# The output norm of a gated-DeltaNet layer in two groups of heads, and the first two output tiles fed head by head

## The reference, cut to what matters

```python
o, s_new = _gated_delta_chunked(q, k, v, g, beta, s0)          # 8 heads of 128
o = _rms_norm(o.astype(h.dtype), o_norm) * jax.nn.silu(gate.reshape(bsz, t_len, H_A, DV))
return o.reshape(bsz, t_len, H_A * DV) @ w_out, new_conv, s_new.astype(h.dtype)
# the caller: x = x + y, then the norm of x and the FFN
```

## Time and profile before

| | |
|---|---|
| median of 3 runs | 2751.65 us |
| the three runs | 2749.22, 2751.65, 2757.39 us |
| the profiled execution | 2749.38 us |
| its span from first to last instruction | 2747.6 us |
| mean granted clock of TensorE | 0.992 |
| busy: TensorE, weight loads, VectorE, ScalarE, GpSimd | 98%, 95%, 48%, 34%, 11% |

### The profile page before, as it was taken

One profiled execution on the slowest core, in us unless ns is written; L12 is line 12 of the kernel. 1 busy time (PEld: TensorE's weight loads), 2 busy tenths in 40 slices (PEclk: granted clock), 3 DMA queues, 4 the chain that ended last, 5 costly groups with the idle time before them and its releaser, 6 DMA issues.

```text
span 2747.6 us, 52338 instructions
## 1 busy us (share of the span) xinstructions
PE 2702.4 (98%) x22041; PEld 2609.8 (95%) x22041; DVE 1327.1 (48%) x1715; ACT 921.6 (34%) x1384; POOL 292.2 (11%) x348
## 2 busy tenths in 40 slices
PE   8999999999999999999999999999999999999999
PEld 8999999998887999999999999999986699999999
DVE  4434347765555643333564343434547754343354
ACT  4222124454323332222342222212348732122243
POOL 2000002211224100000110000000133210000011
PEclk9999999999999999999999999999999999999999
DMA  5223222221012232323222332322303422232321
GB/s 141 77 80 88 77 80 88 87 82 30 20 34 76 83 92 77 92 77 89 84 78 85 121 113 77 92 77 84 105 18 108 142 74 84 82 86 78 87 92 54
DMA packets 308138, 225.96 MB, mean 82 GB/s; under 512 B 8270, under 2 KB 301567, under 8 KB 307967
## 3 DMA queue, kind: packets, MB, share of 16 engines
q1 hardware_dynamic: 307280, 224.26, 27.1%
q0 software_dynamic: 576, 0.00, 0.0%
q10 hardware_dynamic: 162, 0.04, 0.0%
HBM read 212.14 MB, written 12.13 MB: 82 GB/s over the span
## 4 chain that ended last, share of the span: by engine, by line
PE 95%; DVE 3%; issue 1%; ACT 1%; POOL 1%; DVEq 0%; POOLq 0%; ACTq 0%
PE ps L537 80%; PE ps L2445 1%; PE ps L556 1%; PE ps L2411 1%; PE ps L1810 1%; PE ps L2453 1%; PE ps L2350 1%; PE ps L1814 1%; PE ps L1558 0%; PE ps L2595 0%; PE ps L2447 0%; PE ps L2448 0%; DVE w_lo L489 0%; PE ps L1660 0%; PE ps L1833 0%
## 5 line engine op out<-in xcount | busy, mean ns | idle before, releaser
L537 PE MATMUL ps<-hx_hi,w_lo 128*128 128x320 f32 (+1 forms) x3730 | 1096.5, 294 | 0.0
L537 PE MATMUL ps<-hx_lo,w_hi 128*128 128x320 f32 (+1 forms) x3730 | 1096.0, 294 | 0.0
L537 PE MATMUL ps<-hx_hi,w_hi 128*128 128x320 f32 (+1 forms) x3730 | 1089.6, 292 | 1.6 <-DVE w_lo L489 1.3
L474 ACT ACTIVATE w_hi<-raw 128x1024 fp32r<-128x1024 f32 (+1 forms) x362 | 375.4, 1037 | 1216.9 <-PE ps L537 1216.2
L537 PEld LDWEIGHTS ps<-hx_hi,w_hi 128*128 128x128 f32 x3730 | 700.2, 188 | 4.7 <-DVE w_lo L489 2.5
L537 PEld LDWEIGHTS ps<-hx_hi,w_lo 128*128 128x128 f32 x3730 | 700.2, 188 | 0.0
L537 PEld LDWEIGHTS ps<-hx_lo,w_hi 128*128 128x128 f32 x3730 | 699.0, 187 | 0.3
L537 PE MATMUL ps<-hid_hi,w_hi 128*128 128x320 f32 (+1 forms) x1920 | 566.5, 295 | 2.2 <-DVE hid_lo L2239 0.5
L537 PE MATMUL ps<-hid_lo,w_hi 128*128 128x320 f32 (+1 forms) x1920 | 567.6, 296 | 0.0
L537 PE MATMUL ps<-hid_hi,w_lo 128*128 128x320 f32 (+1 forms) x1920 | 561.3, 292 | 0.0
L489 DVE TENSOR_TENSOR w_lo<-raw,w_hi 128x1024 fp32r<-128x1024 f32 (+1 forms) x362 | 460.9, 1273 | 108.7 <-ACT w_hi L474 108.6
(11 more groups left out here) (500 smaller groups left out, 2316.7 us busy)
## 6 DMA issues: line engine op xcount, KB each, us to landing
raw<-in_ffn_w_in SPq DMA_DIRECT2D x176, 512.0 KB, 5.0
raw<-in_ffn_w_out SPq DMA_DIRECT2D x64, 512.0 KB, 4.1
raw<-in_a_w_in SPq DMA_DIRECT2D x33, 512.0 KB, 4.6
raw<-in_ffn_w_out SPq DMA_DIRECT2D x32, 384.0 KB, 3.5
raw<-in_ple_w_gate SPq DMA_DIRECT2D x8, 1024.0 KB, 5.2
raw<-in_w_kv SPq DMA_DIRECT2D x16, 512.0 KB, 4.1
k_page<-in_cache_k SPq DMA_DIRECT2D x16, 512.0 KB, 3.6
v_page<-in_cache_v SPq DMA_DIRECT2D x14, 512.0 KB, 4.7
```

What stands on the lines that cost most here:

```text
L474: nc.scalar.activation(w_hi[:, m, 0:k], s.view(m, slot), ACT.Copy).then_inc(w_hi_done, 1)
L537: last = nc.tensor.matmul(TILE[m][:, c0:c1], w[:, m, k], h[:, k, c0:c1], start=k == 0 and a == 0, stop=k == k_all - 1 and a == 2)
```

## The change

The norm's sums, roots, reciprocals and scales are made for the two groups of heads one after the other, with buffers of their own (`std_c`, `rs_c`, `inv`, the sums' banks). For the first group, the sums are taken in the last level of the last pair, and everything up to the scales within the last scan. The second group follows behind the scan. The update of state 7 writes banks 2 and 5 and waits for the first group's scales where it waited for state 3. The table of the square root is loaded ahead of the last pair's first level. The first two tiles of the output product are fed head by head by `first_products`: a block of tile 0 and a block of tile 1 as the heads come, with transposes and spreads of the second group between them. VectorE's order is written out to match. The 15 matmuls of `keep_warm`, in three calls, become one call with 6. `tail_products` goes.

```diff
-        ... "vnt3_s os3_s upd6_s vnc3_s vnm3_s osum3_s vnm7_s upd3_s upd7_s orec0 orec1 ilo0 ilo1")
+        ... "vnt3_s os3_s orec_a0 orec_a1 upd6_s vnc3_s vnm3_s osum3_s vnm7_s upd3_s ilo_a0 ilo_a1 upd7_s "
+            "orec_b0 orec_b1 ilo_b0 ilo_b1")
...
+        O_SUMS = [[ps[:, b, 0:HC] for b in banks] for banks in ((2, 5), (6, 7))]
+        SPREAD_BANK = (4, 5, 4, 5, 7, 4, 5, 7)
+        O_TOKEN_BANK, O_ROWS_BANK, O_TOKEN_COL = (5, 6), (5, 7), 256
...
 # SyncE
-            after(sp, "su3_s")
+            after(sp, "om3_s")
             load_unit(sp, plan[plan.index(s) + 1], 0, 0)
-            states_out(3)
+            states_out(3, last_state_out)
             after(sp, "su7_s")
             load_unit(sp, plan[plan.index(s) + 1], 0, 1)
-            states_out(7, last_state_out)
+            states_out(7, stored)
...
 # ScalarE
+                if hp == NG - 1:
+                    nc.scalar.preload_act_table_set("sqrt_and_others")
...
+                    if (hp, level) == (NG - 1, LEVELS - 1):
+                        output_sums_read(0)
...
                         o_square(2)
+                        output_roots(0)
+                    if (hp, i) == (NG - 1, 2):
+                        after(act, "osum3_s")
+                        o_square(3)
+                        output_scales_high(0)
...
+            output_high(0, "n0", "s0")
+            output_sums_read(1)
+            split_hi(act, (next_step, 0, 0), 1)
+            output_high(1, "n1", "s0")
+            output_roots(1)
+            output_high(4, "n4", "s4")
+            output_scales_high(1)
+            output_high(5, "n5", "s4")
+            for h in LAST_SUMS:
+                output_high(h, f"n{h}", f"s{h // 4 * 4 + 2}")
...
 # VectorE
+                    if (hp, i) == (3, 3):
+                        sample_update(3)
+                        output_scales_low(0)
...
                     if (hp, i) == (3, 1):
+                        output_reciprocals(0)
                         sample_update(6)
...
+            output_samples(0, 3, 0)
+            output_samples(4, 3, 2 * TS)
+            output_normed(0)
             split_lo(dve, (next_step, 0, 0), 0)
+            output_normed(1)
+            output_low(0)
+            output_normed(4)
+            output_low(1)
+            split_lo(dve, (next_step, 0, 0), 1)
+            output_reciprocals(1)
+            output_normed(5)
+            output_low(4)
+            output_scales_low(1)
+            output_low(5)
+            output_normed(2)
+            output_samples(2, 6, 0)
+            output_samples(6, 6, 2 * TS)
+            output_normed(3)
+            output_low(2)
+            output_normed(6)
+            output_low(3)
+            output_normed(7)
+            output_low(6)
+            output_low(7)
...
 # TensorE, between the tiles of the product
+        def first_products(pe, s):
+            n, base = s.n["unit"], s.n["hid"] - KD
+            blocks = {m: 0 for m in range(2)}
+            def block(m, h):
+                pe.wait_ge(w_lo_done, 2 * n + m + 1)
+                if m:
+                    pe.wait_ge(g["of"], of_count["s4"])
+                    after(pe, "upd7_s")
+                pe.wait_ge(hid_done, base + SQUARED.index(h) + 1)
+                for c0, c1 in PARTS:
+                    for a, (w, x) in enumerate(((w_hi, hid_hi), (w_lo, hid_hi), (w_hi, hid_lo))):
+                        last = nc.tensor.matmul(TILE[m][:, c0:c1], w[:, m, h], x[:, h, c0:c1],
+                                                start=blocks[m] == 0 and a == 0, stop=blocks[m] == KD - 1 and a == 2)
+                blocks[m] += 1
+                if blocks[m] == KD:
+                    last.then_inc(tile_done, 1)
+            block(0, 0)
+            block(0, 1)
+            output_scale_rows(pe, 1)
+            block(0, 4)
+            block(1, 0)
+            block(1, 1)
+            after(pe, "ostd_b1")
+            sample_norm_spread(pe, 1, 6)
+            norm_spread(pe, 4)
+            block(0, 5)
+            block(1, 4)
+            norm_spread(pe, 5)
+            block(1, 5)
+            norm_spread(pe, 6)
+            block(0, 2)
+            block(1, 2)
+            norm_spread(pe, 7)
+            for h in (3, 6, 7):
+                for m in range(2):
+                    block(m, h)
...
 # TensorE, in the last pair
                         sample_update(2, 2)
+                        output_sums(pe, 0)
...
                         sample_read(3)
+                        output_by_token(pe, 0)
                         sample_update(2, 6)
...
                         sample_update(3, 3)
+                        output_scale_rows(pe, 0)
                     if (hp, i) == (3, 3):
-                        after(pe, "osum3_s")
-                        output_sums(FIRST_SUMS, 0)
                         sample_update(3, 7)
-            output_sums(LAST_SUMS, 1)
-            keep_warm(pe, 3, 0)
...
+            sample_norm_spread(pe, 0, 3)
             norm_spread(pe, 0)
-            sample_norm_spread(pe)
-            for h in range(1, 5):
-                norm_spread(pe, h)
+            after(pe, "upd7_s")
+            norm_spread(pe, 1)
+            after(pe, "upd3_s")
+            output_sums(pe, 1)
+            norm_spread(pe, 2)
+            output_by_token(pe, 1)
+            norm_spread(pe, 3)
+            keep_warm(pe, 6, 0)
...
-            tail_products(pe)
```

More of the change, by code:

```diff
@@ L1208, in gdn_act @@
             act.wait_ge(g["ocp"], PT * HA)
-            after(act, "osum2_s", "osum3_s")
-            for h in (3, 6, 7):
+            for h in (6, 7):
                 o_square(h)
-            act.wait_ge(g["osum"], 2)
-            done("osums", nc.scalar.activation(halves(o_sums[:]), O_SUMS, ACT.Copy))
             next_step = plan[plan.index(s) + 1]
-            after(act, "su7_s")
             split_hi(act, (next_step, 0, 0), 0)
[L1217 to L1229, removed]
+            output_high(0, "n0", "s0")
[6 more added lines that the diff above has]
+            output_high(5, "n5", "s4")
+            for h in LAST_SUMS:
+                output_high(h, f"n{h}", f"s{h // 4 * 4 + 2}")
         def gdn_dve(dve, s):
@@ L1535, in sample_norm_spread, with output_sums @@
                                         start=True, stop=True)
-            done("o_sample_scales", last)
+            done(f"o_samples_{'ab'[n]}", last)
+        of_count.update((name, n + 1) for n, name in enumerate("s0 s4 n0 n1 n4 n5 n2 s2 s6 n3 n6 n7".split()))
+        og_count = {h: n + 1 + n // 4 for n, h in enumerate(SQUARED)}
+        def output_sums(pe, n):
+            pe.wait_ge(g["osq"], 4 * n + 4)
+            for half in range(2):
+                for x, h in enumerate((FIRST_SUMS, LAST_SUMS)[n]):
+                    last = nc.tensor.matmul(O_SUMS[n][half][32 * x:32 * x + 32], hot[:, 15 - h:47 - h], osq[h][:, half * HC:(half + 1) * HC],
+                                            start=True, stop=True)
+            last.then_inc(g["osum"], 1)
@@ new lines, in output_by_token, with output_scale_rows @@
+        def output_by_token(pe, n):
+            x = "ab"[n]
+            after(pe, f"osums_{x}")
+            for i in range(NT):
+                rows_, c0 = x_rows_of(i), O_TOKEN_COL + HA * i
+                last = nc.tensor.matmul(bank(O_TOKEN_BANK[n])[0:rows_, c0:c0 + HA], o_sums[:, i * P:i * P + rows_], e32[:, 0:HA],
+                                        start=True, stop=True)
+            done(f"o_by_token_{x}", last)
+        def output_scale_rows(pe, n):
+            x = "ab"[n]
+            after(pe, f"orec_{x}0", f"orec_{x}1")
+            nc.tensor.transpose(bank(O_ROWS_BANK[n])[0:32, 0:P], rs_c[n][:, 0:PT * HA], ident[:])
+            done(f"o_scale_rows_{x}", nc.tensor.transpose(bank(O_ROWS_BANK[n])[0:HA, P:P + TS], rs_c[n][0:TS, PT * HA:], ident[0:TS, 0:TS]))
@@ L1819, in gdn_pe @@
                     after(pe, f"zero{a}")
+                    if hp == NG - 1:
+                        after(pe, "osums_a")
                     for i in range(PT):
```

204 lines of the change are left out of this document (98 added, 106 removed).

## The result

The changed kernel took 2757.0 us at the median of 12 runs (2753.11 to 2761.79), the kernel before 2752.38 (12 runs on the same chip). The ratio is 1.0019, with a 95% interval of 1.0010 to 1.0027: 4.6 us, or 0.19%, slower. That lies inside the 0.3% that were named as no change and got the highest chance, but on the other side of the old time from the forecast of 2749.8, and on the upper end of its range. The profiled execution of the changed kernel took 2757.05 us, 1.7 us more than its span.

What follows compares the result with a forecast made beforehand. TensorE (PE) was taken as the bound, with 95% of the chain. Terms -3.2 + 1.7 + 0.8 - 1.2 = -1.9 us against the profiled 2749.38, carried over to the 2751.65 median, gave 2749.8 us; range 2743.5 to 2757.

Steps and rivals of the forecast that it cites:

- Up to the last scan step: From the table load to the last scan's start: load +0.2, first group's sums +1.11, clock fall gone -1.79; sum -0.47 us.
- The fall at 866.6: Low clock behind a quiet stretch in the inversion: taken as gone because sums fill it, -1.79 us; +1.3 if it stays.
- From state 7 to the first product: Update of state 7 at 887.9, then spreads, last sums and fillers; first product at 896.3 against 899.73 before.
- The stretch from 892.0 to 894.8: Thin work ahead of the first product: a clock fall given one in two, for 1.6 us, so 0.8 counted.
- two signs of being wrong: Between unit 0 and unit 1, PE does not rest; or blocks take 1.6 us throughout.
- the upper bound: Whole kernel: costs of 5 us at both quiet stretches instead of 1.7 and 0.8, giving 2757 us.
- The tiles: First product to tile 0's end: blocks 11.8, spreads 2.0, sample spread 0.43, transposes 0.40, wait 0.15; 14.8 us.
- Between the units: Unit 0 to unit 1: exposed 4.80 us chain to split weights, PE rests 4.1, clock fall behind it costs 1.7.
- The end: Kernel's end: without the tail of 60 matmuls the last store sets the end, -1.2 us, between 0 and -1.4.
- the filling is hidden: Rival, between units: unit 1's weights split before tile 0 completes, no rest or fall; -7.8 us, 2743.9; chance 0.14.
- the clock stays low through the fed tiles: Rival, first two tiles: low clock from 894.8 until tile 0 ends, +10 us, 2762; chance 0.10.
- VectorE's queue: Rival, first two tiles: VectorE's 16 us queue sets their end, so nothing moves; 1 us delay gives 2751; chance 0.14.

Runs made afterwards that it cites:

- a1: Changed kernel with the tail of 60 matmuls at the end put back; 2757.12 us, ratio 1.0016 to the kernel before.
- a2: Changed kernel with tile 0 of the output product completed before tile 1 begins; 2754.05 us, ratio 1.0003 to the kernel before.
- b4: Changed kernel with its last two loops exchanged, so tile 0 ends three blocks ahead of tile 1; 2756.84 us, ratio 1.0013 to the kernel before.
- a4: Changed kernel with ten fillers around the last sums and behind the sums by token, replacing six at the end; 2753.67 us, ratio 1.0002 to before.
- b1: Changed kernel with tile 0 completed before tile 1 and the ten fillers moved as in a4; 2749.7 us, ratio 0.9993 to the kernel before.
- b2: As b1, but two blocks of tile 1 put into PE's wait ahead of tile 0's head 2 block; 2748.76 us, ratio 0.9989 to before.
- c2: The same kernel as b2, run once more; 2749.28 us, ratio 0.9990 to the kernel before.
- a3: Kernel before with tile 0's last block moved behind tile 1's seventh, so both tiles end together; 2755.6 us, ratio 1.0008 to the kernel before.
- c1: Kernel before without its tail of 60 matmuls, nothing else changed; 2750.11 us, ratio 0.9997 to the kernel before.

## Why the prediction was wrong

**Up to the last scan step it held.** The table load took 1.28 and the copy began 1.32 behind S where it had begun 1.07 behind it: 0.25 late, forecast 0.21. The Trainium skill's drain of 1.38 us beside a load (ScalarE: Activation LUTs, What ACT_TABLE_LOAD costs) did not appear here: the copy started 0.02 us behind the load. The sums cost 1.11. The fall at 866.6 was taken as gone. In the changed kernel it was, and L1974, the former L1821, took 2.07 instead of 3.58, 0.28 more than the 1.79 in the sum. But it came back in a1, a2 and b4, where state 7's update lies 51.0 behind S. So the sums don't end that fall. It came in three of nine profiles with the new scan and in three of three with the old, too few to say that they make it rarer; when it comes it costs 3.0 us of the new scan's time.

**From state 7 to the first product is where the prediction failed.** The step is "The stretch from 892.0 to 894.8 is thin as well; I give a fall there one in two, for 1.6: 0.8". The clock fell earlier, in the sums themselves or the spread ahead of them, in every profile that has the fillers where the change put them or none, and stayed low for about 10 us and not for one short stretch. From state 7 to the first product the forecast was 8.4 and the measurement 11.5. a4 gives the size: 9.1, with four fillers more, each 0.28 of a microsecond (four took 1.12), so 8.0 like for like if all four stand in PE's row, and 3.5 for the fall up to there. The steps of the chain give about the same: the last sums took 0.4 more than in a4, the two spreads 0.9, the sums by token 0.9 and six fillers 1.2, together 3.4. In the tiles it cost another 1.1 (17.4 against 16.3). Together 4.6 where 0.8 stood. PE was busy 2.94 of the 3.30 us ahead of the fall, so idle time alone did not announce it: what PE did there were spreads (64 rows), 32-column sums and short steps of the scan. The prediction read the earlier trace rows rightly as a clock that falls behind such work and then gave the same kind of work, moved forward, only a small price. Of the two signs of being wrong that it named, no rest between the units and blocks of 1.6 us throughout, neither came. That the median lies on the edge of the range is luck in part: the upper bound allowed 5 us for each of two quiet stretches, where 4.6 and 1.6 were used, and nothing for the blocks and spreads, which took 1.5 more.

**The tiles.** 14.8 was forecast, and 16.3 came even at full clock (a4). The fifteen blocks took 13.1, not 11.8: those behind a spread or a transpose take 0.98 and not 0.79, and the sum used the mean of a dense tile for all. Spreads took 0.59 there and not 0.50. 1.5 us are missing from the sum. That VectorE keeps ahead of PE was right for this order, at full clock too (a4); in a2, b1, b2, c2 and b4, with other orders, PE waits for it 0.6 to 1.2 us.

**Between the units it held.** The chain was forecast at 4.80 and took 4.76 (921.98 to 926.74), PE rested 4.3 where 4.1 was said, and the low stretch behind it took 3.4 us and cost 1.6, forecast 1.7. The rule that the prediction cited (the Trainium skill, TensorE: Matmul & The Clock Gate, Why this matters for your kernels) warns of idle gaps between bursts. The trace agrees for this fall, behind a rest of 4.3 us, and for the one behind b4's rest of 2.7 us. It does not cover the fall that cost most, where PE was busy 2.94 of 3.30 us, nor b1's first one. The prediction took the old fall at 900.7 as agreeing with it; that one, too, came behind a window with PE busy 2.85 of 3.30 us, and not behind a rest.

**The end.** SyncE's two waits fell from 4.8 to 3.8, 1.0 against 1.2 forecast. a1 and a3 show that the 1.4 us which the term took off is not there in every execution with the tail, and c1's interval holds nothing as well as 1.2. The term is not shown.

**The sum, mended.** From state 7 to the eighth tile, forecast 8.4 + 14.8 + 4.95 + 39.7 + 0.8 = 68.6; measured 73.5. The difference of 4.9 is +3.8 for the fall, +1.5 for blocks and spreads, and -0.4 for a first part that without the fall would have taken 8.0.

**The rivals.** That the filling is hidden was wrong for this order. In b2 it is hidden but for 0.4 us, not because the weights are split before tile 0 is complete but because tile 1's blocks stand behind it. That the clock stays low through the fed tiles was half right: it was low, but back at 907.1, when 2.5 us of products had run, and the price was 4.6 and not 13. VectorE's queue did not bound the tiles here; in a2, b1, b2, c2 and b4 it cost a wait of 0.6 to 1.2 us.

**What stays open.** The edited stretch is 4.0 us longer and the end 1.0 shorter, 3.0 together; the medians stand 4.6 apart, and the interval begins at 2.8. The missing 1.6 us lie within the scatter of the low stretches elsewhere, which came to 5.38 us ahead of S in this one profile, but no run assigns them. The experiments rank the same way in both measures: from changed over a4 and b1 to b2 the stretch falls by 3.5, 5.6 and 8.3 us and the time, by the ratios, by 4.7, 7.2 and 8.3. But a3's median rose by 2 us where its stretch rose by 5 to 6. Open, too, are what set off b1's first low stretch and what moved fillers would give the kernel before.

## What to carry to other kernels

A block order that feeds two output tiles at once makes them complete at once. Where one buffer for each tile's weights is refilled only behind the tile, the refill chain is then exposed: leave most of a tile's work behind the first tile's end (b2), and put only as many blocks of the second ahead as cover a real wait. Fillers belong between the thin matmuls, ahead of where the clock falls; six behind the fall took 2.9 us and kept nothing (the stretch was 1.4 shorter without them), and ten spread over the thin stretch in their place gained 3.5 net. Try them in the old order first, before that order is changed. When short matmuls are moved, carry along the low clock that stood behind them at the old place, and price the work behind them at it.

## What the runs showed that was not expected

The clock fell at the last sums while PE was busy 2.94 of 3.30 us, and did not fall there once three fillers stood ahead of them and seven behind; in b1 it then fell at the first product, with PE busy 3.40 of 3.40 us. A wait of 1.2 us for one low part was followed by low stretches of 6.8 us (a2) and 3.4 us (b1), although PE had been busy 5.72 of 5.80 us ahead of it in a2; a wait of 0.6 us in b2 and c2 was followed by none.

A block of six matmuls took 0.98 us behind a 64-row spread and 0.79 within a dense tile, both at full clock.
